# Three more size classes, from 232 columns up, for the expert items of a one-core hybrid decoder step

## What is computed

```python
logits = xt @ w_router                              # 1,088 tokens, 8 experts
top_v, top_i = lax.top_k(logits, 2)                 # each token goes to two experts
...                                                 
h  = silu(x_e @ wg[e]) * (x_e @ wu[e])              # 1,024 -> 3,584, for the rows of expert e
ys = (h @ wd[e]) * softmax(top_v)                   # 3,584 -> 1,024, added back to the tokens
```

## Time and profile before

| what | us |
|---|---|
| median of three runs | 5345.38 |
| lowest and highest of them | 5335.77 and 5347.17 |
| the profiled execution, its own time | 5342.29 |
| its span in the trace | 5340.7 |
| mean granted clock of TensorE, as a share of full speed | 0.967 |

### The profile page before, as it was taken

The page is one execution under the profiler, slowest core; times in us unless marked ns, Lnnn a source line. Parts: engine busy times, 40 slices in busy tenths (PEclk is TensorE's granted clock), DMA queues, the critical chain, the costliest instruction groups (busy, mean ns, idle before and its releaser), DMA issues. The chain is left out here.

```text
span 5340.7 us, 86721 instructions
## 1 busy us (share of the span) xinstructions
PE 5028.7 (94%) x33128; PEld 4946.9 (93%) x33129; DVE 3410.5 (64%) x5291; ACT 1601.9 (30%) x2280; POOL 403.4 (8%) x246
## 2 busy tenths in 40 slices
PE   8999999999998999999969898999999898989969
PEld 7999999999998999999869898998999898989958
DVE  5677756544447666865657576565667676766665
ACT  2112222111113211122234343333334444433333
POOL 3111101011102211110010000000000000000020
PEclk8999999999999999999979999999999999999979
DMA  3111111111111111111055454444445455544431
GB/s 98 45 43 39 41 45 40 40 48 41 47 48 38 52 41 44 47 41 39 19 201 180 142 165 146 145 142 141 156 158 187 164 183 169 183 152 144 147 115 40
DMA packets 399015, 528.60 MB, mean 99 GB/s; under 512 B 12056, under 2 KB 353606, under 8 KB 398616
## 3 DMA queue, kind: packets, MB, share of 16 engines
q1 hardware_dynamic: 359552, 460.75, 26.1%
q0 software_dynamic: 11136, 33.97, 1.9%
q10 hardware_dynamic: 27928, 28.60, 1.6%
HBM read 494.87 MB, written 28.39 MB: 98 GB/s over the span
## 5 line engine op out<-in xcount | busy, mean ns | idle before, releaser
L1478 DVE TENSOR_TENSOR WLO<-WRAW,WHI 128x1024 fp32r<-128x1024 f32 x866 | 1065.6, 1232 | 292.4 <-ACT WHI L1110 177.1
L659 PE MATMUL PS<-XHI,WHI 128*128 128x384 f32 (+1 forms) x3648 | 1202.5, 330 | 3.7 <-DVE ACC L1987 2.1
L661 PE MATMUL PS<-XHI,WLO 128*128 128x384 f32 (+1 forms) x3648 | 1197.0, 328 | 0.0
L660 PE MATMUL PS<-XLO,WHI 128*128 128x384 f32 (+1 forms) x3648 | 1196.5, 328 | 0.0
L1110 ACT ACTIVATE WHI<-WRAW 128x1024 fp32r<-128x1024 f32 x866 | 899.0, 1051 | 984.2 <-PE PS L765 732.0
L659 PE MATMUL PS<-XSH,WHI 128*128 128x256 f32 (+5 forms) x3584 | 1071.3, 299 | 45.9 <-issue 37.8
L660 PE MATMUL PS<-XSL,WHI 128*128 128x256 f32 (+5 forms) x3584 | 1068.6, 298 | 2.0 <-issue 2.0
L661 PE MATMUL PS<-XSH,WLO 128*128 128x256 f32 (+5 forms) x3584 | 1065.7, 297 | 0.0
L659 PEld LDWEIGHTS PS<-XSH,WHI 128*128 128x128 f32 x3584 | 682.0, 190 | 50.0 <-issue 46.2
L659 PEld LDWEIGHTS PS<-XHI,WHI 128*128 128x128 f32 x3648 | 691.0, 189 | 7.1 <-DVE ACC L1987 2.9
L660 PEld LDWEIGHTS PS<-XLO,WHI 128*128 128x128 f32 x3648 | 690.8, 189 | 0.7
(11 more groups left out here) (367 smaller groups left out, 5770.6 us busy)
## 6 DMA issues: line engine op xcount, KB each, us to landing
WRAW<-in_moe_w_gate SPq DMA_DIRECT2D x112, 1024.0 KB, 5.0
WRAW<-in_moe_w_up SPq DMA_DIRECT2D x112, 1024.0 KB, 5.0
WRAW<-in_moe_w_down SPq DMA_DIRECT2D x112, 1024.0 KB, 4.9
WRAW<-in_w_in SPq DMA_DIRECT2D x48, 1024.0 KB, 5.2
WRAW<-in_ffn_w_gate SPq DMA_DIRECT2D x11, 1024.0 KB, 5.3
WRAW<-in_ffn_w_up SPq DMA_DIRECT2D x11, 1024.0 KB, 5.3
WRAW<-in_ffn_w_down SPq DMA_DIRECT2D x11, 1024.0 KB, 4.9
XG<-sorted_rows POOLq DMA_DIRECT2D x18, 512.0 KB, 4.6
```

The lines of the kernel that those rows point to most:

```text
L659: pe.matmul(PS[:, bank, 0:n], wh, hi(k), start=(k == 0), stop=False)
L660: pe.matmul(PS[:, bank, 0:n], wh, lo(k), start=False, stop=False)
L661: ins = pe.matmul(PS[:, bank, 0:n], wl, hi(k), start=False, stop=(k == KC - 1))
L1478: v.do(dve.tensor_tensor(WLO[s][:], raw_view(conv.n // 2 % RAW, conv.n % 2, kind), WHI[s][:].bitcast(F32), ALU.subtract), conv)
```

## The change

```diff
 MOE_GROUPS = DFE // 256
 XBLK = ((0, 128), (128, 128), (256, CAP - 256))
-SIZES = tuple(range(256, CAP + 1, 8))
+SIZES = tuple(range(232, CAP + 1, 8))
 LIST = SLOTS + 2
```

## The result

The changed kernel takes 5298.83 us (median of four runs, 5294.93 to 5304.34), the kernel before 5340.58 beside it: ratio 0.9922, 95% interval 0.9904 to 0.994. That is 42 us faster. The profiled execution took 5294.93 us (span 5293.3).

What follows compares the result with a forecast made beforehand. The prediction took TensorE's matmuls to bound the kernel; -27.8 (narrow matmuls) + 2.4 (wider matmuls) + 2.7 (jumps) = -22.7 us from the median 5345.4 gave 5323 us, range 5303 to 5358.

Steps and rivals of the forecast that it cites:

- What bounds it: Whole kernel: TensorE, busy 94% of the span, sets the time; an item lasts as long as its 2,016 matmuls.
- The narrow matmuls: Items 4 and 6: 232-column matmuls start 111.6 ns apart, as bare weight loads do, not 118.75; 27.8 us saved.
- no floor: Rival, items 4 and 6: weight loads never show, a 232-column matmul costs 108.75 ns; 5312 us in all; chance 0.13.
- nothing gained: Rival, items 4 and 6: 118.75 ns is already the weight load's floor; 5350 us in all; chance 0.21.
- a slow mode: Rival, items 4 and 6: matmuls below 256 columns run at a slower rate, near 5650 or 6415 us; chance 0.18.
- the clock: Rival, items 4 and 6: TensorE waiting for loads drops to half clock, some 430 us more; chance 0.02.
- The wider matmuls: Items 0, 1, 3 and 5: new class boundaries add 5,760 columns in all, 2.4 us more.
- the list: Loop at line 2100: three more rounds, 1.3 us, hidden before GpSimd loads the first rows, so no cost.
- VectorE: Item groups: its unchanged work has 2.46 us of waits for TensorE, so a group shortened by 1.0 us still fits.
- The jumps: TensorE's branches choosing a size: one level more at 2.7 us, so 2.7 us more, with 8 us to either side.
- The sum: Whole kernel: the terms together give -22.7 us, 5323 us predicted; chance 0.46.

## Why the prediction was wrong, point by point

- *What bounds it* was right: TensorE's matmuls, and two items of eight narrowed.
- *The narrow matmuls*: right to the nanosecond. 111.6 ns was taken from bare weight loads and 111.5 was measured; 27 us were forecast for the columns of items 4 and 6 against the same tree at 256, and 26 to 29 came. The rivals *no floor* (108.75), *nothing gained* (118.75), *a slow mode* and *the clock* all fall, by the counts in 150 us. By the total alone *no floor* (5312) would have looked nearest. Both the columns and the weight load set the spacing: 118.4 ns at 256 columns follows the columns, 111.5 ns at 232, 216 and 128 is the 111.6 ns of the bare loads. *A slow mode* would have shown at 240 columns already, and there the spacing went on falling, to 112.2 ns; for *the clock*, the granted clock was 1.00 in every one of these stretches.
- *The wider matmuls* (+2.4) and *the list* (nothing): not contradicted, too small to see by themselves. *VectorE*: right in item 4's groups, the cover held. Its waits on EACC at the ends of items were read as VectorE's own; at least in part they are the jumps on the way up under another name.
- *The jumps*: this is the step that failed. I divided 74.8 us of waits by 28 levels, took 2.7 us for every level and counted one level more: +2.7, with 8 us to either side. The runs showed -16 for the tree at equal columns (5326.1 - 5340.6 - 1.8; -12 to -25 by the ratio's interval), 19 us from the +2.7. The waits are not spread evenly over the levels, so an average could give neither the sign nor the size: another split with two levels more was 7 us faster, and 6 of the 16 us lie in the wait after the last item, 13.1 us by "issue" in the profile before, just behind the stretch that I had summed. I had also kept the spread at 8 us, three waits' worth of an average, although single waits in the earlier trace rows reach 5.3 us and the new tree changes the path of four of the eight items.
- *The sum*: -27.8 + 2.4 + 2.7 became -42. The direction held by the first term; the size is off by the third. By what rule a jump is cheap or dear stays open.

## What to carry to other kernels

Here a matmul of 4-byte data with 128 columns of weights cost 0.417 ns a moving column and 12 ns down to 240 columns (112.2 ns), and 111.5 ns at 232, 216 and 128; pad or split with that in mind, and look for the floor in a chain of weight loads with a tiny moving operand in the same trace, which here had 111.6 ns from one to the next. When a program has one copy of its body for each size, count the branches and their order as a cost of their own: here seven copies instead of fourteen were worth 25 to 27 us, of which columns were 3, nearly as much as the narrow matmuls. An average over waits of one kind is no price for adding one more of them; try the same tree with the old sizes first, since it splits such a change in two.

## What the runs showed of the hardware that was not expected

- The knee between 240 and 232 columns is sharp, start to start: 118.4 ns at 256 columns, 112.2 at 240, 111.5 at 232, 216 and 128. The duration that the profile shows for a matmul does not tell this: 281 ns at 256, 275 at 232, and only the distance of the starts does.
- A jump over 1,200 instructions ahead of each item, in front of a wait, cost nothing (ratio 0.9996), while at a jump inside the tree TensorE idled up to 5.3 us (item 1 of the profile before).
- Whole trees moved by 64 or 128 instructions changed the time by 0.1% at most (ratios 0.9999 and 0.999 to the kernel before, and 0.9926 where the changed kernel had 0.992).
- After a wait of 5.22 us at a jump the granted clock was 0.50 for 5 us.
- The granted clock was 1.00 from 4000 to 4150 us with only 128 columns in each 111.5 ns.
